# Block two: tile 0 turned inside the sum of tile 1, two units multiplied tile by tile, and a fourth place for high halves

## What is computed

```python
def second_block(x, positions, w_in, ..., w_out, ln1_g, ln1_b, w_ff1, w_ff2, ln2_g, ln2_b):
    for l in range(DEPTH):                                   # DEPTH = 2
        mix = mixer_sublayer(x, positions, w_in[l], ..., w_out[l])
        x = layer_norm_2(DEEPNORM_ALPHA_2 * x + mix, ln1_g[l], ln1_b[l])
        ff = jnp.square(jax.nn.relu(x @ w_ff1[l])) @ w_ff2[l]   # 1024 -> 4096 -> 1024
        x = layer_norm_2(DEEPNORM_ALPHA_2 * x + ff, ln2_g[l], ln2_b[l])
    return x
```

## Time and profile before

| | |
|---|---|
| median of 3 runs | 1674.12 us (1673.54 to 1674.95) |
| span of the profiled execution, first to last instruction | 1675.9 us |
| mean granted TensorE clock | 0.991 |
| TensorE matmuls busy | 1635.3 us (98%) |
| VectorE / ScalarE busy | 890.5 us / 721.8 us |
| read from HBM | 409.52 MB |

### The profile page before, as it was taken

The page is one execution under the profiler, slowest core; times in us unless marked ns, Lnnn a source line. Parts: engine busy times, 40 slices in busy tenths (PEclk is TensorE's granted clock), DMA queues, the critical chain, the costliest instruction groups (busy, mean ns, idle before and its releaser), DMA issues.

```text
span 1675.9 us, 25227 instructions
## 1 busy us (share of the span) xinstructions
PE 1635.3 (98%) x10724; PEld 1285.9 (77%) x10724; DVE 890.5 (53%) x1190; ACT 721.8 (43%) x1084; POOL 32.6 (2%) x56
## 2 busy tenths in 40 slices
PE   8999999998999999997999999999999999999998
PEld 7878644435988644434989998989989899988997
DVE  7777421104677411104658656655566676575555
ACT  4775211112675211113655544544456564444443
POOL 0000000000000000000000000000000000000000
PEclk9999999998999999998999999999999999999999
DMA  9637999997837999997745565555556455555552
GB/s 270 230 126 283 353 416 418 416 417 255 269 134 271 357 416 418 417 417 273 218 136 175 176 202 176 193 184 185 192 157 199 134 169 177 201 192 185 185 192 76
DMA packets 193109, 413.07 MB, mean 246 GB/s; under 512 B 16416, under 2 KB 130848, under 8 KB 176608
## 3 DMA queue, kind: packets, MB, share of 16 engines
q1 hardware_dynamic: 191904, 409.81, 68.3%
q10 hardware_dynamic: 1088, 1.57, 0.4%
HBM read 409.52 MB, written 1.84 MB: 245 GB/s over the span
## 4 chain that ended last, share of the span: by engine, by line
PE 90%; DVE 3%; DMA 3%; ACT 2%; issue 1%; SPq 1%; POOL 0%; ACTq 0%; DVEq 0%
PE PS L1700 13%; PE PS L513 11%; PE PS L517 11%; PE PS L514 11%; PE PS L521 9%; PE PS L525 9%; PE PS L524 9%; PE PS L1723 5%; DMA weights_raw<-in_w_in 3%; PE PS L540 2%; PE PS L1676 2%; PE PS L1732 2%; DVE hT_lo L729 1%; DVE weights_low L493 1%; ACT arena L863 0%
## 5 line engine op out<-in xcount | busy, mean ns | idle before, releaser
L493 DVE TENSOR_TENSOR weights_low<-weights_raw,weights_hi 128x1024 fp32r<-128x1024 f32 x368 | 431.2, 1216 | 199.7 <-ACT weights_hi L488 198.8
L488 ACT ACTIVATE weights_hi<-weights_raw 128x1024 fp32r<-128x1024 f32 x368 | 365.7, 1046 | 136.6 <-PE PS L525 66.6
L513 PE MATMUL PS<-hT_hi,weights_hi 128*128 128x256 f32 (+1 forms) x1456 | 411.4, 283 | 0.9 <-ACT bias L955 0.9
L517 PE MATMUL PS<-hT_hi,weights_low 128*128 128x256 f32 (+1 forms) x1456 | 409.6, 281 | 1.4 <-DVE weights_low L493 1.4
L514 PE MATMUL PS<-hT_lo,weights_hi 128*128 128x256 f32 (+1 forms) x1456 | 409.2, 281 | 0.0
L513 PEld LDWEIGHTS PS<-hT_hi,weights_hi 128*128 128x128 f32 (+1 forms) x1456 | 274.6, 189 | 4.8 <-issue 2.7
L517 PEld LDWEIGHTS PS<-hT_hi,weights_low 128*128 128x128 f32 (+1 forms) x1456 | 274.8, 189 | 2.0 <-DVE weights_low L493 1.8
L514 PEld LDWEIGHTS PS<-hT_lo,weights_hi 128*128 128x128 f32 (+1 forms) x1456 | 274.8, 189 | 1.2
L525 PE MATMUL PS<-weights_hi,opa_lo 128*128 128x512 f32 x384 | 152.6, 397 | 0.0
L521 PE MATMUL PS<-weights_hi,opa_hi 128*128 128x512 f32 x384 | 152.4, 397 | 0.2
L524 PE MATMUL PS<-weights_low,opa_hi 128*128 128x512 f32 x384 | 151.0, 393 | 0.0
(11 more groups left out here) (335 smaller groups left out, 2367.7 us busy)
## 6 DMA issues: line engine op xcount, KB each, us to landing
weights_raw<-in_w_in SPq DMA_DIRECT2D x80, 1024.0 KB, 5.5
weights_raw<-in_w_ff SPq DMA_DIRECT2D x64, 1024.0 KB, 5.2
arena<-in_w_down SPq DMA_DIRECT2D x22, 1024.0 KB, 22.8
arena<-in_w_gate SPq DMA_DIRECT2D x20, 1024.0 KB, 15.0
weights_raw<-in_w_up SPq DMA_DIRECT2D x20, 1024.0 KB, 17.3
weights_raw<-in_w_gate SPq DMA_DIRECT2D x20, 1024.0 KB, 17.6
arena<-in_w_up SPq DMA_DIRECT2D x16, 1024.0 KB, 13.7
weights_raw<-in_w_down SPq DMA_DIRECT2D x16, 1024.0 KB, 16.0
```

What stands on the lines that cost most here:

```text
L488: act.activation(u.flat[0][:, c:e], u.x[:, c:e], ACT.Copy).then_inc(*sig.mark("w_hi", u.u, i))
L493: dve.tensor_tensor(u.flat[1][:, c:e], u.x[:, c:e], u.flat[0][:, c:e].bitcast(F32), ALU.subtract).then_inc(*sig.mark("w_lo", u.u, i))
L513: pe.matmul(o, w[0], x[0], start=start, stop=False)
L517: return pe.matmul(o, w[1], x[0], start=False, stop=stop)
```

## The change

Four things, all in the second block.

1. `accumulate_rows` gets `late`: the turn of tile 0 is issued inside the sum of tile 1, ahead of the last 6 of its 24 matmuls (the last half of the last unit). VectorE takes tile 0's turn ahead of tile 1's sum instead of behind it (`turned_early`).
2. `project_two_by_tiles` takes two units (ff1 0 and ff1 1, or gla v0 and gla v1 of layer 1): tile 0 of both, then tile 1 of both. Tile 1's two halves are turned within the second unit's tile 0, ahead of its k = 6 and its k = 7. The filler matmuls are gone. In the feed-forward both units are by rows and both are turned, under ff1 2. gla v0 and gla v1 of layer 0 stay as they were.
3. The plan of the feed-forward puts ff1 two stages ahead: ff1 0, ff1 1, ff1 2, ff2 0, ff1 3, ff2 1, ...
4. High halves get a fourth place, in memory that the first block's experts used. From gla v0 of layer 0 on, `feed` splits up to three units behind the one in use, and a high place comes free with the unit four before.

The core of the diff:

```diff
         cols("ff1 0", a["w_ff1_2"][l], 0)
+        cols("ff1 1", a["w_ff1_2"][l], 256)
         for i in range(16):
-            if i + 1 < 16:
-                cols(f"ff1 {i + 1}", a["w_ff1_2"][l], 256 * (i + 1))
+            if i + 2 < 16:
+                cols(f"ff1 {i + 2}", a["w_ff1_2"][l], 256 * (i + 2))
             rows(f"ff2 {i}", a["w_ff2_2"][l], 256 * i)
...
+            ring = [NRAW + (second_block + i) % NSPLIT for i in range(NSPLIT)] + [AT_OWN[0]]
...
-                    self.split_until(self.used + NSPLIT)
+                    self.split_until(self.used + (MORE_SPLIT if self.used >= second_block else NSPLIT))
...
                             for k in range(u.k):
+                                if late is not None and sp and t and half and k == 0:
+                                    late()
...
+        def project_two_by_tiles(pe, names, x, by, norm):
+
+            b = [banks.take(pe, name, by, among=4) for name in names]
+            for t in range(NT):
+                for i, name in enumerate(names):
+                    u = units[place[name]]
+                    if t == 0:
+                        use(pe, name)
+                    for k in range(KD):
+                        if t == 0 and i == 1 and k >= KD - 2:
+                            turn_half(pe, norm, 1, k - (KD - 2))
+                        if i == 0 and k % 4 == 0:
+                            pe.wait_ge(*sig.at("dve_took", f"{norm} T{t}{k // 4}"))
+                        last = rows_still(pe, PS[:, b[i], t * S:(t + 1) * S], u, at_k(x, k, t * P, (t + 1) * P),
+                                          at_k(u.pair, k, 0, S), k == 0, k == KD - 1, t == k == 0)
+                    if t == NT - 1:
+                        last.then_inc(*sig.mark("ps", name))
...
-        def norm_vector(dve, label, scale, turned=True, within=None):
-            for t in range(NT):
+        def norm_vector(dve, label, scale, turned=True, within=None, turned_early=False):
+            for t in range(NT):
+                if t and turned_early:
+                    turned_lo(dve, label, 0)
                 dve.wait_ge(*sig.at("ps", f"{label} t{t}"))
...
-            project_tiles(pe, L("ff1 0"), hT, "act_took", among=4, norm=n_("ln1b"))
+            project_two_by_tiles(pe, L("ff1 0", "ff1 1"), hT, "act_took", n_("ln1b"))
...
-            for i in range(N_STAGE):
-                if i + 1 < N_STAGE:
-                    project_T(pe, L(f"ff1 {i + 1}"), hT, "act_took", among=4, between=turn_first() if i == 0 else None)
-                if i < N_STAGE - 2:
-                    pe.wait_ge(*sig.at("ff_dve", n_(f"up {i}")))
-                    accumulate_rows(pe, L(f"ff2 {i}"), opa, 2 * (i % 4), n_("ln2b"), i == 0, False)
+            for i in range(N_STAGE - 2):
+                project_T(pe, L(f"ff1 {i + 2}"), hT, "act_took", among=4, between=turn_rows() if i == 0 else None)
+                pe.wait_ge(*sig.at("ff_dve", n_(f"up {i}")))
+                accumulate_rows(pe, L(f"ff2 {i}"), opa, 2 * (i % 4), n_("ln2b"), i == 0, False)
...
+            for i in range(N_STAGE):
+                if i + 2 < N_STAGE:
+                    feed(n_(f"ff1 {i + 2}"))
+                act.wait_ge(*sig.at("ps", up_of(i)))
+                if i > 1:
+                    act.wait_ge(*sig.at("ff_dve", n_(f"up {i - 2}")))
+                act.activation(relu_t[i % 2], one_bank(banks.of(up_of(i)), 2), ACT.Relu).then_inc(
+                    *sig.mark("act_took", up_of(i)))
```

More of the change, by code:

```diff
@@ L423, in assign_places, with dense_before @@
             return found
-        before_experts = [sum(not of_expert(p[0]) for p in plan[:place[f"ple gate 3 {l}"] + 1]) for l in range(DEPTH)] + [len(plan)]
+        def dense_before(u):
+            return sum(not of_expert(p[0]) for p in plan[:u])
+        before_experts = [dense_before(place[f"ple gate 3 {l}"] + 1) for l in range(DEPTH)] + [len(plan)]
+        second_block = dense_before(place["gla v0 0"])
         unit_place = assign_places()
@@ L604, in project_rows, with accumulate_rows @@
             sig.also("ps", f"{label} t1")
-        def accumulate_rows(pe, names, x, k_of, label, first, final, ready=(), turns=False, midway=None):
+        def accumulate_rows(pe, names, x, k_of, label, first, final, ready=(), turns=False, midway=None, late=None):
             groups = [(n,) for n in names[:-2]] + [names[-2:]] if turns else [(n,) for n in names]
@@ L767, in norm_vector @@
                     dve.wait_ge(*sig.at("params_in", label))
-                elif turned:
+                elif turned and not turned_early:
                     turned_lo(dve, label, 0)
@@ L2140, in tensor_block2 @@
             n_ = lambda name: f"{name} {l}"
-            project_tiles(pe, L("gla v0"), hT, "act_took", among=4, norm="ln2 1" if l == 0 else "ln2b 0")
-            project_tiles(pe, L("gla v1"), hT, "act_took")
+            if l == 0:
+                project_tiles(pe, L("gla v0"), hT, "act_took", among=4, norm="ln2 1")
+                project_tiles(pe, L("gla v1"), hT, "act_took")
+            else:
+                project_two_by_tiles(pe, L("gla v0", "gla v1"), hT, "act_took", "ln2b 0")
             project_T(pe, L("gla q0", "gla q1"), hT, "act_took")
@@ new lines, in turn_rows @@
+            def turn_rows():
+                for i in range(2):
+                    b = banks.take(pe, n_(f"ff1 {i} turned"), "act_took", among=4)
+                    pe.wait_ge(*sig.at("act_took", n_(f"ff1 {i}")))
+                    for t in range(NT):
+                        for c in range(2):
+                            last = transpose(pe, PS[:, b, c * S + t * P:c * S + (t + 1) * P], by_rows[i][:, t, c * P:(c + 1) * P])
+                    last.then_inc(*sig.mark("ps", n_(f"ff1 {i} turned")))
+                    yield
@@ new lines, in scalar_block2 @@
+            up_of = lambda i: n_(f"ff1 {i}" if i > 1 else f"ff1 {i} turned")
+            for i in range(2):
+                feed(n_(f"ff1 {i}"))
+                act.wait_ge(*sig.at("ps", n_(f"ff1 {i}")))
+                copy(by_rows[i], PS[:, banks.of(n_(f"ff1 {i}")), :].rearrange("p (t n) -> p t n", t=NT)).then_inc(
+                    *sig.mark("act_took", n_(f"ff1 {i}")))
+            for i in range(N_STAGE):
[6 more added lines that the diff above has]
+                    *sig.mark("act_took", up_of(i)))
+                act.wait_ge(*sig.at("ff_dve", n_(f"square {i}")))
+                if i > 3:
+                    act.wait_ge(*sig.at("ps", n_(f"ff2 {i - 4}")))
+                q = 2 * (i % 4)
+                hi_part(act, opa[0][:, q:q + 2, :], relu2[i % 2]).then_inc(*sig.mark("ff_act", n_(f"up {i}")))
+                if i < N_STAGE - 2:
+                    feed(n_(f"ff2 {i}"))
@@ L2411, in scalar_block2 @@
+            feed(n_(f"ff2 {N_STAGE - 2}"))
             norm_scalar(act, n_("ln2b"), turned=l + 1 < DEPTH)
```

90 lines of the change are left out of this document (36 added, 54 removed).

## The result

The changed kernel takes 1684.89 us (median of 4, 1682.44 to 1685.54), the kernel before 1674.53 us beside it. The ratio is 1.0055, with a 95% interval from 1.0043 to 1.0067. I had forecast 1676 us, with a range that ended at 1681.

A forecast was written before the change was run, and what follows sets the result against it. TensorE, busy 98% of the span, was taken as the bound, with gains only at three turns. The sum -2.17 - 2 x 0.20 + 4.4 = +1.8 us on 1674.12 gave about 1676, range 1669.5 to 1681.

The forecast's parts named there:

- The turn of ln2b 0: Turn ahead of gla v0 and gla v1: both done at 1241.43 instead of 1243.60, 2.17 us won.
- The turn of ln1b without later waits: Turn ahead of the feed-forward, twice: each wins 1.53 us if nothing else waits.
- What is late next, up 0: At ff2 0, up 0 comes 1.23 us late plus 0.10 of restart, leaving 0.20 of 1.53 for each ln1b.
- What may be late in every stage: Feed-forward stages 1 to 13, two layers: relu queued behind a blocked split loses 0.17 us a stage, 4.4 in all.
- edits at no cost: Mixer splits and loads cost nothing; at layer 0's start a short bank would cost 2 us, once.
- The rival of the clock: With the filler gone the clock falls; three turns would lose 6.9 us on top, 1683; chance 0.03.

The follow-up runs named there:

- relu_first: Changed kernel with the split of ff1 i+2 moved behind stage i's relu and halves on ScalarE and VectorE; 1667.29 us, 0.9948 of the kernel before.
- own_banks: Changed kernel with the two turned stages back in their own units' PSUM banks (0 and 1); 1676.87 us, 1.0006 of the kernel before.
- filler: Changed kernel with 9 filler matmuls into a free PSUM bank ahead of ff1 4, in both layers; 1681.60 us, 1.0037 of the kernel before.
- fourth_place_only: Kernel before with only the fourth high place and splits three units ahead in the second block; 1675.65 us, 0.9998 of the kernel before.
- relu_first_no_late: relu_first with tile 0 turned behind tile 1's sum, as in the kernel before, no filler; 1671.05 us, 0.9969 of the kernel before.
- relu_first_turn_at_5: relu_first with tile 1's halves turned ahead of k = 5 and 6 instead of 6 and 7; 1666.71 us, 0.9941 of the kernel before.

## Why the prediction was wrong, point by point

- **The turn of ln2b 0** (2.17 won): right, 2.1 in the changed kernel. The waits are in the places named but shorter: 0.25 ahead of tile 0's transposes (I had 0.40, and 0.67 at ln1b, where it is 0.25 too), none listed between their halves (0.22), 0.25 ahead of tile 1's product (0.47). One working in it is wrong: 48 matmuls in 5.70 less 0.03 are 0.118 each and not 0.1195. The size held all the same, since 42 matmuls of a product by tiles, with no other between them, take 5.04, which is 0.120 each.
- **The turn of ln1b without later waits** (1.53): 1.73 in relu_first, where nothing waits behind it.
- **What is late next, up 0** (1.23 and 0.10 of restart): right in place and nearly in size. The view lists 1.00 in both layers. From start to start it is 1.15 in layer 1: tile 0's sum to ff2 0 takes 27.52 (1479.77 to 1507.29), against 26.38 in relu_first.
- **What may be late in every stage** (0.17): right. A stage went from 11.29 to 11.45 on average (1545.62 to 1660.12 are ten stages). The rule that the queues of ScalarE and VectorE are strictly in order ("TensorE: Matmul & The Clock Gate" of the Trainium skill, Architectural detail) is borne out: relu starts 1.91 behind a split that TensorE's end of ff2 releases (1524.70 to 1526.61), though its input, ff1 2, was done before ff2 0 (1507.29), some 20 us earlier and not 5 as I wrote. Of the 4.4 us that I had for this, 3.5 were lost against before (22 x 0.16), 5.0 against relu_first. (0.08 and 0.10 make 0.18 and not 0.17, which changes nothing.)
- **The step that failed is "edits at no cost" and, in "what is late next", its end.** I followed one consumer of the blocked relu, up i, and not the other: the PSUM bank that it frees. The only word on banks in the prediction was about layer 0's first product. Two turned stages now take two of the four banks, so ff1 4 comes two products behind ff1 2 in the same bank, and relu of stage 2 is then needed at the start of ff1 4 instead of its end. I had this term at nothing; it measured 2.73 us of waiting in each layer, with 1.59 and 1.28 of lower clock behind it. own_banks takes both away by the banks alone.
- **The rival of the clock** had the right mechanism at the wrong place and with a reason against it that doesn't hold: "my longest wait is 1.2 us" was no longer so. It cost 1.59 us in layer 0 and 1.28 in layer 1, and filler gave 1.4 and 0.7 back with TensorE starting no sooner.

By steps, for layer 1: -1.73, +1.10 (up 0 with its restart), +2.73, +1.28, and 0.16 for 11 stages (+1.8) make +5.2, measured +5.0. Over the whole, 8.1 of the 8.5 us by which the stretches grew go with own_banks, which takes away just the two terms that I didn't have. My sum of the rest was +1.8. own_banks is at 1.0006 of before, 1.0 us more with an interval from -0.5 to +2.7, and 0.4 more by the stretches: the rest of the sum lies within the noise of this, and by the stretches it was a little too dear.

What stays open: in relu_first a stage takes 11.22 us on average (1501.72 to 1524.15 are two in 22.43), 0.07 less than before, with no wait in either. ff1 has a pitch (time from start to start of its matmuls) of 5.64 / 48 = 0.1175 us instead of 0.1188. Over two layers this is some 2 us of its gain of 8.3, so not all of the gain is waits that went. It is not the fourth place (fourth_place_only has 5.70 and 5.59), and it isn't the new order of units either, as the expectation of fourth_place_only had it: own_banks has the new order, and in layer 1 all its products from ff1 3 on have the longer pitch. The changed kernel has both, in turn. Here are the 47th matmuls of ff1 5, which starts at 1539.86, and of ff1 6, which starts at 1551.33:

```profile
1545.26 0.28 PE L522 MATMUL PS<-hT_lo,weights_hi 128*128 128x256 f32 x1
...
1556.79 0.28 PE L522 MATMUL PS<-hT_lo,weights_hi 128*128 128x256 f32 x1
```

46 steps take 5.40 in the one and 5.46 in the other. There the wait ahead of ff2 hides the difference, and both products take 5.76. Kernels with relu first show the longer pitch too, in the first products of a feed-forward (relu_first_no_late and relu_first_turn_at_5 in ff1 3 and ff1 4). What sets the pitch of a product I did not find out.

## What to carry to other kernels

When a wait moves ahead of an instruction in an in-order queue, list everything that instruction releases, not only its result: here the result was 0.1 us late, and the PSUM bank it frees 2.7 us. Put work whose input is long there (relu) ahead of work that waits for a place to come free (a split made three units in advance); the look-ahead can afford to be late, and the same change went from 0.55% slower to 0.52% faster by that order alone, of which some 0.1% is the pitch that stays unexplained. Without cover an early turn and a second unit are worth little one by one (about 0 and 1.3 us a turn), so such parts are to be tried together, with each wait they leave read off the trace.

## What the runs showed of the hardware

- A wait of 2.73 us of TensorE, with the clock at 1.00 before, brought the granted clock to 0.50 for about 3 us and cost 1.28 us beyond the wait in layer 1 and 1.59 in layer 0. 9 filler matmuls in 2.17 us, with 1.05 us of waiting left (0.72 in layer 0), kept it at full rate.
- Waits of 1.57 and 0.75 us within 4 us did so in some executions of a program and not in others, at the same place.
- The first matmul behind a wait that is too short for the profile to list still shows: 0.34 us to the next instead of 0.24.
- Products of 48 matmuls of 256 columns ran at one of two steady pitches, 5.40 or 5.46 us for 46 steps at full clock, and changed from one to the other between products of one execution.
